# Pooling as fp32 products with averaging matrices, and rows of features turned on TensorE and fetched back from DRAM

## The chip, the cores and the metric

The kernel runs on one core of a Trainium2 chip. The metric is the device time in microseconds of one execution of the program; the time shown is the median of three runs. The profile is one further execution. TensorE appears as PE (matmuls) and PEld (weight loads), VectorE as DVE, ScalarE as ACT, GpSimd as POOL and SyncE as SP.

## The reference

Two small transformers follow one another on 256 tokens of 1024 features. The first has two layers (sparse attention, then differential attention) and a final norm, the second two layers: a pooling mixer, then block attention, each modulated by vectors that come from a conditioning vector `c` and the matrix `w_mod`. The change lies at the seam between them, in the pooling mixer and in what makes rows of modulation vectors:

```python
def modulate(h, shift, scale):
    return h * (1 + scale[:, None, :]) + shift[:, None, :]

def pool_mixer(h, w_pool, pool_scale):
    ...
    for g, w in enumerate(POOL_WINDOWS):          # 2, 4, 8, 16
        sl = slice(g * POOL_GROUP, (g + 1) * POOL_GROUP)
        cs_g = cs[:, :, sl]                       # running sums over tokens
        lo = jnp.maximum(t + 1 - w, 0)
        win_sum = cs_g[:, 1:] - jnp.take(cs_g, lo, axis=1)
        cnt = jnp.minimum(t + 1, w).astype(jnp.float32)[None, :, None]
        groups.append(win_sum / cnt - hf[:, :, sl])
    pooled = jnp.stack(groups, axis=2)
    y = jnp.einsum('bsgi,gio->bsgo', pooled, w_pool.astype(jnp.float32)).reshape(B, S, D)
    return (y * pool_scale.astype(jnp.float32)).astype(h.dtype)
```

Its input is the final norm of the first model, normed again and modulated; its output is multiplied by a gate and added to the stream `x`.

## The kernel before

Tokens lie in two tiles of 128 (`t`), features in 8 blocks of 128 (`b`). All weights come as one stream of 1 MB chunks through a ring of four buffers; SP issues the loads. ACT makes the upper half of each chunk (`whi`, `hi_upto`), DVE the remainder (`wlo`, `lo_upto`), and PE multiplies in three fp32r products (`three`, L1224). Nothing is scheduled by a planner: each engine's order is the order of its own program text, and semaphores join them.

The stages are: even mixer, MLP0, differential mixer, MLP1, pooling, MLP2, block-attention mixer, MLP3. Norms are numbered as events. Event 4 is the first model's final norm, event 5 the norm ahead of the pooling, event 6 the one ahead of MLP2, events 7 and 8 lie around the last mixer. In an event DVE adds the product to `x` (`residual`, L745, or L747 and L749 with a gate), ACT squares it (L446) and makes `std` (L451), DVE makes `rstd` (L756) and scales rows into `o_` (`scaled`, L762), PE transposes them (`norm`, L1307), ACT scales the features out of PSUM (`upper`, L463 or L465) and DVE splits them (`lower`, L775 and L776). `add_and_norm` (L778) does one tile and then the other.

The pooling stage: after events 4 and 5, PE transposes both tiles, ACT writes features into `qk` with gain and shift, and DVE adds shifted copies of them along the tokens (L1171, L1172), corrects the first tokens (L1175) and subtracts the token itself (L1176), group by group; ACT makes the upper part (L674), DVE the remainder (L1181, L1184), and PE multiplies by the pool's weights. Then follow two `wlo` splits, `mod_vectors(1)` (L820, L824), the residual of event 6 by halves, and its norm.

A vector over features lies as a column, [128, 8]. Where a row on all partitions is needed (the gates, and `cact`, by which DVE multiplies `w_mod` at L791 in MLP0 to MLP2), PE multiplies each broadcast column by the identity (`spread_col`, L1314), 8 fp32 products, and ACT copies two banks (`spread_copy`, L526). This stands in MLP0, MLP2 and MLP3, at the head of the last mixer, and for `gpool` in front of event 5's transposes. `w_mod` is loaded through POOL's queue (L411), one pair of buffers in turn.

## Time and profile before

| | |
|---|---|
| median of three runs | 1220.47 us (1219.09 to 1221.52) |
| profiled execution, its own time | 1216.48 us |
| its span, mean granted clock | 1214.6 us, 0.985 |
| PE busy | 1136.2 us, 94% |
| DVE busy | 812.5 us, 67% |
| ACT busy | 598.5 us, 49% |
| DMA | 248.57 MB, mean 205 GB/s |

The span is cut into 40 slices of 30.4 us. PE is at eight or nine tenths or more in nearly all; the lowest pair is slices 23 and 24 (5 and 6 tenths), where the granted clock is also lower (7 and 8 tenths): the pooling stage. "Clock" is the granted clock as a share of full speed: 1 is 2.4 GHz, 0.5 is 1.2 GHz. Matmul records overlap, so that their durations add up to more than the time they take; the distance between starts is what one costs.

### The profile page before, as it was taken

To read this page: it belongs to the slowest core of one execution; us is meant where nothing else is said; L and a number is where in the kernel's file an instruction comes from. 1 tells how busy PE (TensorE), PEld (TensorE's weight loads), DVE (VectorE), ACT (ScalarE), POOL (GpSimd) and SP (SyncE) were. 2 spreads that over 40 slices of the span, in tenths; PEclk is the share of its full clock that TensorE was granted. 3 is DMA by queue.
4 is the path that set the end of the run, shared out by engine and by line. 5 is a ranking of instruction groups with operands and counts; after the bars stand their busy time and mean duration, and the time that the engine had idled before them with its cause. 6 is when DMAs were issued, how large, how long until landed. Compare 5 with 4: busy or idle time off the path is not lost.

```text
span 1214.6 us, 17892 instructions
## 1 busy us (share of the span) xinstructions
PE 1136.2 (94%) x7264; PEld 986.2 (81%) x7264; DVE 812.5 (67%) x1342; ACT 598.5 (49%) x930; POOL 53.3 (4%) x103
## 2 busy tenths in 40 slices
PE   5898999999999999999999569999999998999997
...
DMA packets 36274, 248.57 MB, mean 205 GB/s; under 512 B 4560, under 2 KB 4704, under 8 KB 7520
## 3 DMA queue, kind: packets, MB, share of 16 engines
...
## 4 chain that ended last, share of the span: by engine, by line
PE 83%; DVE 10%; ACT 4%; issue 2%; DMA 1%; SPq 0%; DVEq 0%; ACTq 0%
PE bank L1229 71%; PE bank L1647 2%; PE bank L1411 2%; PE bank L1436 2%; DVE wlo L729 1%; PE bank L1474 1%; DVE x L749 1%; ACT vo L446 1%; DVE wlo L840 1%; DVE work L747 1%; PE bank L1307 1%; DVE ul L776 1%; PE bank L1630 1%; DMA raw<-in_stream 1%; PE bank L1711 1%
## 5 line engine op out<-in xcount | busy, mean ns | idle before, releaser
L729 DVE TENSOR_TENSOR wlo<-raw,whi 128x2048 fp32r<-128x2048 f32 (+2 forms) x143 | 324.5, 2274 | 108.2 <-ACT whi L436 108.1
L1229 PE MATMUL bank<-uh,whi 128*128 128x256 f32 x1272 | 367.4, 289 | 0.0
L1229 PE MATMUL bank<-ul,whi 128*128 128x256 f32 x1272 | 359.7, 283 | 0.0
L1229 PE MATMUL bank<-uh,wlo 128*128 128x256 f32 x1272 | 359.7, 283 | 0.0
L436 ACT ACTIVATE whi<-raw 128x2048 fp32r<-128x2048 f32 (+2 forms) x143 | 270.6, 1897 | 1.8 <-DMA raw<-in_stream 1.8
L1229 PEld LDWEIGHTS bank<-uh,whi 128*128 128x128 f32 x1272 | 243.5, 191 | 9.2 <-issue 6.7
L1229 PEld LDWEIGHTS bank<-ul,whi 128*128 128x128 f32 x1272 | 243.6, 192 | 4.0 <-issue 1.9
L1229 PEld LDWEIGHTS bank<-uh,wlo 128*128 128x128 f32 x1272 | 243.5, 191 | 0.0
L1229 PE MATMUL bank<-whi,hh 128*128 128x512 f32 x544 | 214.0, 393 | 0.0
L1229 PE MATMUL bank<-wlo,hh 128*128 128x512 f32 x544 | 212.4, 390 | 0.0
L1229 PE MATMUL bank<-whi,hl 128*128 128x512 f32 x544 | 211.8, 389 | 0.0
L494 ACT ACTIVATE hh<-work 128x512 fp32r<-128x512 f32 x56 | 35.4, 632 | 173.2 <-PE bank L1229 173.2
L1229 PEld LDWEIGHTS bank<-whi,hl 128*128 128x128 f32 x544 | 102.1, 188 | 21.8
L1229 PEld LDWEIGHTS bank<-whi,hh 128*128 128x128 f32 x544 | 102.4, 188 | 20.9 <-issue 1.6
L490 ACT ACTIVATE work<-bank 128x512 f32<-128x512 f32 x56 | 33.5, 598 | 174.1 <-PE bank L1229 174.1
L1229 PEld LDWEIGHTS bank<-wlo,hh 128*128 128x128 f32 x544 | 102.4, 188 | 18.8 <-issue 0.2
L791 DVE CUSTOM_DVE_ANT_0 qk<-qk,cb 128x1024 f32<-128x1024 f32 x96 | 113.1, 1221 | 0.0
L1229 PE MATMUL bank<-whi,uh 128*128 128x256 f32 (+2 forms) x256 | 88.4, 345 | 19.6 <-DVE ul L776 10.1
L805 DVE TENSOR_TENSOR work<-work 128x512 f32<-128x512 f32 x56 | 38.7, 691 | 74.5 <-ACT work L490 74.5
L1229 PE MATMUL bank<-wlo,uh 128*128 128x256 f32 (+2 forms) x256 | 85.1, 332 | 0.0
L1229 PE MATMUL bank<-whi,ul 128*128 128x256 f32 (+2 forms) x256 | 85.0, 332 | 0.0
L840 DVE TENSOR_TENSOR wlo<-raw,whi 128x1024 fp32r<-128x1024 f32 x56 | 67.4, 1219 | 8.5 <-ACT whi L617 8.4
(205 smaller groups left out, 1118.2 us busy)
## 6 DMA issues: line engine op xcount, KB each, us to landing
...
bias_rows<-gb POOLq DMA_DIRECT2D x16, 192.0 KB, 9.1
...
x<-in_x SPq DMA_DIRECT2D x2, 512.0 KB, 4.7
vo<-in_fin_g POOLq DMA_DIRECT2D x2, 512.0 KB, 6.7
out_y<-vo SPq DMA_DIRECT2D x2, 512.0 KB, 2.6
```

The costliest lines, as they stand in the source:

```text
L436: nc.scalar.activation(whi[:, c % RING, 0:w], raw[:, n % RING, 0:w], ACT.Copy).then_inc(hi_ready, 1)
L446: nc.scalar.activation(o_[:, t, 512 * h:512 * h + 512], x[:, t, 512 * h:512 * h + 512], ACT.Square, accum_out=ss[:, 2 * t + h:2 * t + h + ...
L490: nc.scalar.activation(work[:, s % 2, :], bank[s % 2][:, :], ACT.Relu).then_inc(relu_done, 1)
L494: nc.scalar.activation(hh[:, s % 2, :], work[:, s % 2, :], ACT.Square).then_inc(hh_done, 1)
L729: nc.vector.tensor_tensor(wlo[:, c % RING, 0:w], raw[:, raw_index(c) % RING, 0:w], whi[:, c % RING, 0:w].bitcast(fp32), ALU.subtract).then ...
L791: ins = nc.vector.tensor_tensor_reduce(out=stage[j][:, r, :], in0=stage[j][:, r, :], in1=cb[:, :], scale=1.0, scalar=0.0, op0=ALU.mult, op ...
L805: nc.vector.tensor_tensor(work[:, 2 + s % 2, :], work[:, s % 2, :], work[:, s % 2, :], ALU.mult)\
L840: ins = nc.vector.tensor_tensor(wlo[:, m % RING, c], raw[:, raw_index(m) % RING, c], whi[:, m % RING, c].bitcast(fp32), ALU.subtract)
L1229: ins = mm(out, st, mv, start=start and i == 0, stop=stop and i == 2, skip_group_check=True)
L1411: ins = mm(bank[3 + c][:, c0:c1], qk[rows_, qb, 128 * t:128 * t + 128], qk[rows_, kb, 0:c1 - c0], start=True, stop=True)
L1436: ins = nc.tensor.transpose(bank[5][:, 128 * k:128 * k + 128], P[:, (2 * p + c) % 4, 128 * k:128 * k + 128], ident)
L1647: ins = mm(bank[acc_of(1)[2 * t + h]][:, :], oT[c][:, k, 128 * t:128 * t + 128], w[:, k, 512 * h:512 * h + 512], start=c == 0 and k == 0, ...
```

## The change

**Pooling.** The averaging over the window, less the token itself, becomes a matrix over tokens. For each of the four groups it is made on the host (`pool_windows`, 128x1152 in all), with the part that carries the last tokens of tile 0 into the first 16 of tile 1. PE multiplies the normalised rows of a tile by it as plain fp32, 8 products of 128 columns a tile and 8 of 16 columns from tile 0 into tile 1, which turns rows into features at the same time. The gain is put on by DVE as it writes the rows (`pool_input`); the shift only matters where a row of the matrix does not sum to nought, the first tokens, and comes as 8 products of one row by 16 columns. The transposes of event 5, the 16 ACT copies into `qk` and DVE's chain of adds go. ACT and DVE take halves of each tile out of PSUM (`pooled_upper`, `pooled_lower`). Tile 0 is done ahead of tile 1, also in the product with the pool's weights and in event 6, which is now `add_and_norm(6, gateb)`. `mod_vectors(1)` moves ahead of event 4; one of the two `wlo` splits stays ahead of event 6, the other moves behind it.

**Rows.** A column is turned by one PE transpose into 8 rows of 128 (three columns in MLP1: `gpool`, the pooling's gain and shift), copied by ACT into `rowb`, written to DRAM and fetched on all partitions by POOL's queue. `cact` is turned in the even mixer, and `gpool` in MLP1.

```diff
-            def spread_col(col, b0):
-
-                for b in range(KB):
-                    ins = mm(bank[b0 + b // 4][:, 128 * (b % 4):128 * (b % 4) + 128],
-                             col[:, b:b + 1].to_broadcast([128, 128]), ident, start=True, stop=True)
-                ins.then_inc(spread, 1)
+            def turn_columns(*cols):
+
+                for n, col in enumerate(cols):
+                    ins = nc.tensor.transpose(bank[6][0:8, 128 * n:128 * n + 128], col, ident)
+                ins.then_inc(row_ps, 1)
...
-            def spread_copy(k, dst, b0):
-                act.wait_ge(spread, k + 1)
-                for j in range(2):
-                    nc.scalar.activation(dst[:, 512 * j:512 * j + 512], bank[b0 + j][:, :], ACT.Copy).then_inc(spread_out, 1)
+            def turned_columns(k, n=1):
+                act.wait_ge(row_ps, k + 1)
+                if k:
+                    act.wait_ge(row_out[k - 1], 16)
+                nc.scalar.activation(rowb[:, 0:n, :], bank[6][0:8, 0:128 * n].rearrange("p (n f) -> p n f", n=n), ACT.Copy)\
+                    .then_inc(row_sb, 1)
...
+            def rows_to(k, n=1):
+
+                pool.wait_ge(row_sb, k + 1)
+                pool.dma_start(rdram[k, 0:n, :].rearrange("n (b p) -> b n p", p=128), rowb[:, 0:n, :]).then_inc(row_out[k], 16)
+
+            def row_from(k, dst, n=0):
+
+                pool.wait_ge(row_out[k], 16)
+                pool.dma_start(dst, rdram[k, n, :].partition_broadcast(128)).then_inc(row_in[k], 16)
...
+                    pool.dma_start(win[:, 0:W_END], a["windows"]).then_inc(in_win, 16)
...
+                    if m == 1 and i == 2:
+                        rows_to(1, 3)
+                    elif m == 1 and i == 4:
+                        row_from(1, gateb)
+                        row_from(1, gain_row, 1)
+                        pool.dma_start(shift_row, rdram[1, 2:3, :]).then_inc(row_in[1], 16)
+                    elif m == 2 and i == 2:
+                        rows_to(2)
+                    elif m == 2 and i == 4:
+
+                        pool.wait_ge(x_ready, x_no(6, 1, 1))
+                        row_from(2, gateb)
...
-            for t in range(NT):
-                deviation(4, (t,))
-                deviation(5, (t,))
-            spread_copy(1, gateb, 2)
-            act.wait_ge(mod_ready, 1)
-            for t in range(NT):
-                upper(5, t, gain[:, 0, :], mod[:, 0:8], qk[:, 0:8, :])
-            hi_upto(POOL + 3)
-            for g in range(4):
-                act.wait_ge(p_sum, g + 1)
-                nc.scalar.activation(uh[:, 2 * g:2 * g + 2, :], u[:, 2 * g:2 * g + 2, :], ACT.Copy).then_inc(p_hi, 1)
-            deviation(6, halves=(0,))
-            deviation(6, halves=(1,))
+            def pooled_upper(t):
+
+                for h in range(2):
+                    act.wait_ge(p_sum, 2 * t + h + 1)
+                    nc.scalar.activation(uh[:, 4 * h:4 * h + 4, 128 * t:128 * t + 128],
+                                         bank[2 * t + h][:, :].rearrange("p (b n) -> p b n", b=4), ACT.Copy).then_inc(p_hi, 1)
+
+            deviation(4, (0,))
+            deviation(5, (0,))
+            deviation(4, (1,))
+            pooled_upper(0)
+            deviation(5, (1,))
+            pooled_upper(1)
+            hi_upto(POOL + 2)
             act.wait_ge(mod_ready, 2)
             for t in range(NT):
+                deviation(6, (t,))
                 upper(6, t, gain[:, 1, :], mod[:, 24:32])
+            hi_upto(POOL + 3)
             mlp(2)
             for t in range(NT):
...
+            mod_vectors(1)
+            dve.wait_ge(row_in[1], 48)
+
+            def pool_input(t):
+
+                inverse(5, t)
+                for q in range(4):
+                    c = slice(256 * q, 256 * q + 256)
+                    nc.vector.scalar_tensor_tensor(out=o_[:, t, c], in0=x[:, t, c], scalar=rstd[:, t:t + 1], in1=gain_row[:, c],
+                                                   op0=ALU.mult, op1=ALU.mult).then_inc(xs_ready, 1)
+
+            def pooled_lower(t):
+                for h in range(2):
+                    dve.wait_ge(p_hi, 2 * t + h + 1)
+                    us_ = slice(4 * h, 4 * h + 4), slice(128 * t, 128 * t + 128)
+                    nc.vector.tensor_tensor(ul[:, us_[0], us_[1]], bank[2 * t + h][:, :].rearrange("p (b n) -> p b n", b=4),
+                                            uh[:, us_[0], us_[1]].bitcast(fp32), ALU.subtract).then_inc(p_h, 1)
+
             for t in range(NT):
                 residual(4, (t,))
                 inverse(4, t)
                 gained(4, t, x, x_ready)
-                scaled(5, t)
-
-            hb, sa = qk[:, 0:8, :], qk[:, 8:16, :]
-            sbb = P[:, :, :].rearrange("p a n -> p (a n)").rearrange("p (b n) -> p b n", n=T)
-            dve.wait_ge(un_ready, un_no(6, 0))
-            for g, w in enumerate((1, 2, 4, 8)):
-                n = 8 - 2 * g
-                src = (hb, sa[:, 2:8, :], sbb[:, 2:6, :], sa[:, 6:8, :])[g]
-                dst = (sa, sbb, sa[:, 4:8, :], sbb[:, 4:6, :])[g]
-                nc.vector.tensor_copy(dst[:, 0:n, 0:w], src[:, 0:n, 0:w])
-                link(nc.vector.tensor_tensor(dst[:, 0:n, w:T], src[:, 0:n, w:T], src[:, 0:n, 0:T - w], ALU.add))
-
-                cor = con[:, C_CORR + 32 * g:C_CORR + 32 * g + 32].rearrange("p (b n) -> p b n", b=2)
-                link(nc.vector.tensor_tensor(dst[:, 0:2, 0:16], dst[:, 0:2, 0:16], cor, ALU.mult))
-                nc.vector.scalar_tensor_tensor(out=u[:, 2 * g:2 * g + 2, :], in0=dst[:, 0:2, :],
-                                               scalar=1.0 / (2 << g), in1=hb[:, 2 * g:2 * g + 2, :],
-                                               op0=ALU.mult, op1=ALU.subtract).then_inc(p_sum, 1)
-                if g:
-                    dve.wait_ge(p_hi, g)
-                    nc.vector.tensor_tensor(ul[:, 2 * g - 2:2 * g, :], u[:, 2 * g - 2:2 * g, :],
-                                            uh[:, 2 * g - 2:2 * g, :].bitcast(fp32), ALU.subtract).then_inc(p_h, 1)
-            dve.wait_ge(p_hi, 4)
-            nc.vector.tensor_tensor(ul[:, 6:8, :], u[:, 6:8, :], uh[:, 6:8, :].bitcast(fp32), ALU.subtract).then_inc(p_h, 1)
-            lo_upto(POOL + 3)
-            mod_vectors(1)
-            dve.wait_ge(spread_out, 4)
-            residual(6, halves=(0,), gate=gateb)
-            residual(6, halves=(1,), gate=gateb)
-            for t in range(NT):
-                scaled(6, t)
-            for t in range(NT):
-                lower(6, t)
+                if t:
+                    pooled_lower(0)
+                pool_input(t)
+            pooled_lower(1)
+            lo_upto(POOL + 2)
+            add_and_norm(6, gateb)
...
-                if l == 0:
-                    pe.wait_ge(col_ready, 2)
-                    spread_col(cact, 6)
+                if l == 1:
+                    pe.wait_ge(mod_ready, 1)
+                    turn_columns(gpool[:, :], gain[:, 0, :], mod[:, 0:8])
                 elif l == 2:
                     pe.wait_ge(mod_ready, 2)
-                    spread_col(mod[:, 40:48], 6)
+                    turn_columns(mod[:, 40:48])
                 elif l == 3:
                     pe.wait_ge(mod_ready, 3)
-                    spread_col(mod[:, 88:96], 6)
+                    turn_columns(mod[:, 88:96])
...
-                if l != 1:
-                    pe.wait_ge(spread_out, (2, 0, 6, 10)[l])
+                if l:
+                    pe.wait_ge(row_sb, (0, 2, 3, 5)[l])
...
-            pe.wait_ge(mod_ready, 1)
-            spread_col(gpool, 2)
-            pe.wait_ge(spread_out, 4)
-            for t in range(NT):
-                norm(5, t)
-
+
+            pe.wait_ge(in_win, 16)
+            pe.wait_ge(row_in[1], 48)
+
+            for b in range(KB):
+                c = W_SUM + WIDEST * (b // 2)
+                mm(bank[b // 4][:, 128 * (b % 4):128 * (b % 4) + WIDEST], shift_row[0:1, 128 * b:128 * b + 128],
+                   win[0:1, c:c + WIDEST], start=b % 4 == 0, stop=False, skip_group_check=True)
+
+            def pooled(t, c0, n, to=None):
+
+                to = t if to is None else to
+                for b in range(KB):
+                    if b % 2 == 0:
+                        pe.wait_ge(xs_ready, 4 * (dg_no(5, t) - 1) + b // 2 + 1)
+                    c = W_GROUP * (b // 2) + c0
+                    ins = mm(bank[2 * to + b // 4][:, 128 * (b % 4):128 * (b % 4) + n], o_[:, t, 128 * b:128 * b + 128],
+                             win[:, c:c + n], start=to > t and b % 4 == 0, stop=True, skip_group_check=True)
+                    if b % 4 == 3 and to == t:
+                        ins.then_inc(p_sum, 1)
+
+            pooled(0, 0, 128)
+            pooled(0, W_NEXT, WIDEST, 1)
             pe.wait_ge(lo_ready, POOL + 1)
             wp = [w[:, POOL % RING, :].rearrange("p (g k n) -> p g k n", g=4, k=2) for w in (whi, wlo)]
-            for g in range(4):
-                pe.wait_ge(p_h, g + 1)
-                for t in range(NT):
-                    ts = slice(128 * t, 128 * t + 128)
+            for t in range(NT):
+                ts = slice(128 * t, 128 * t + 128)
+                if t:
+                    pooled(1, W_SECOND, 128)
+                for g in range(4):
+                    pe.wait_ge(p_h, 2 * t + g // 2 + 1)
                     for k in range(2):
                         ins = three(bank[4 + 2 * t + g // 2][:, 256 * (g % 2):256 * (g % 2) + 256], False,
                                     wp[0][:, g, k, :], wp[1][:, g, k, :], uh[:, 2 * g + k, ts], ul[:, 2 * g + k, ts],
                                     g % 2 == 0 and k == 0, g % 2 == 1 and k == 1)
-                    if g == 1 or (g == 3 and t == 0):
+                    if g % 2 and (t, g) != (1, 3):
                         ins.then_inc(acc_ready, 1)
             ins.then_inc(used, 1)
...
+def pool_windows():
+    win = np.zeros((128, W_END), np.float32)
+    s, t = np.arange(T)[:, None], np.arange(T)[None, :]
+    for g in range(4):
+        w = 2 << g
+        weight = np.where((t >= s) & (t - s < w), np.float32(1) / np.minimum(t + 1, w).astype(np.float32), np.float32(0))
+        weight = weight - np.eye(T, dtype=np.float32)
+        c = W_GROUP * g
+        win[:, c:c + 128] = weight[:128, :128]
+        win[:, c + W_NEXT:c + W_SECOND] = weight[:128, 128:128 + WIDEST]
+        win[:, c + W_SECOND:c + W_GROUP] = weight[128:, 128:]
+
+        win[0, W_SUM + WIDEST * g:W_SUM + WIDEST * g + WIDEST] = weight.astype(np.float64).sum(0)[:WIDEST]
+    return win```

The order of the instructions, at three places. First DVE around the end of event 5, before: the rows `vo` of tile 1, then the adds along the tokens (`qk` and `P` are scratch for features).

```order
L753 TENSOR_SCALAR bias<-ss 128x1
L756 RECIPROCAL rstd<-std 128x1
L762 TENSOR_SCALAR vo<-x,rstd 128x256 x4
L1171 COPY qk<-qk 128x8
L1172 TENSOR_TENSOR qk<-qk 128x8x255
L1175 TENSOR_TENSOR qk<-qk,con 128x2x16
L1176 SCALAR_TENSOR_TENSOR u<-qk 128x512
L1171 COPY P<-qk 128x6x2
L1172 TENSOR_TENSOR P<-qk 128x6x254
L1175 TENSOR_TENSOR P<-P,con 128x2x16
L1176 SCALAR_TENSOR_TENSOR u<-P,qk 128x512
L1181 TENSOR_TENSOR ul<-u,uh 128x512
```

And DVE now, from tile 1's residual of event 4 to the first gate product of event 6 (`work<-bank,vo`):

```order
L797 TENSOR_TENSOR x<-bank,x 128x512 x2
L805 TENSOR_SCALAR bias<-ss 128x1
L808 RECIPROCAL rstd<-std 128x1
L819 SCALAR_TENSOR_TENSOR x<-x,rstd,vo 128x512 x2
L1225 TENSOR_TENSOR ul<-bank,uh 128x4x128 x2
L805 TENSOR_SCALAR bias<-ss 128x1
L808 RECIPROCAL rstd<-std 128x1
L1218 SCALAR_TENSOR_TENSOR vo<-x,rstd,u 128x256 x4
L1225 TENSOR_TENSOR ul<-bank,uh 128x4x128 x2
L781 TENSOR_TENSOR wlo<-raw,whi 128x2048
L799 TENSOR_TENSOR work<-bank,vo 128x512
L801 TENSOR_TENSOR x<-work,x 128x512
```

The remainder of tile 0 stands between tile 1's two norms, and one `wlo` stands ahead of the gate product. Second, PE at the end of MLP1, before (`con` holds the identity):

```order
L1229 MATMUL bank<-wlo,hh 128x512
L1229 MATMUL bank<-whi,hl 128x512
L1314 MATMUL bank<-con,gpool 128x128 x8
L1307 MATMUL bank<-con,vo 128x128 x16
L1229 MATMUL bank<-whi,uh 128x256
```

And now (`P` holds the window matrices, `u` the row of shifts, `vo` the rows of a tile):

```order
L1273 MATMUL bank<-wlo,hh 128x512
L1273 MATMUL bank<-whi,hl 128x512
L1788 MATMUL bank<-P,u 128x16 x8
L1798 MATMUL bank<-P,vo 128x128 x8
L1798 MATMUL bank<-P,vo 128x16 x8
L1273 MATMUL bank<-whi,uh 128x256
```

The spread and the 16 transposes are replaced by three sets of eight; a fourth set, tile 1's, stands behind tile 0's 24 products with the pool's weights. Third, POOL's queue from the even mixer's end to MLP2, before:

```order
L411 DMA qk<-in_w_mod 128x2048 x16
L400 DMA bias_rows<-gb 128x1x384 x16
L406 DMA vo<-in_fin_g 128x1024
L411 DMA qk<-in_w_mod 128x2048 x32
L418 DMA u<-bias_rows 128x256 x16
```

And now, for MLP1's part:

```order
L433 DMA vo<-in_fin_g 128x1024
L434 DMA P<-in_windows 128x1152
L451 DMA qk<-in_w_mod 128x2048 x2
L395 DMA feature_rows<-rowb 8x3x128
L451 DMA qk<-in_w_mod 128x2048 x2
L400 DMA vo<-feature_rows 128x1024
L400 DMA u<-feature_rows 128x1024
L442 DMA u<-feature_rows 1x16x64
L451 DMA qk<-in_w_mod 128x2048 x14
```

The write of the rows stands behind the first pair of `w_mod` loads, the three fetches behind the second.

## Rows read from the trace of the kernel before

**Rows 1.** The page's chain that ended last: shares of the span by engine

```profile
PE 83%; DVE 10%; ACT 4%; issue 2%; DMA 1%; SPq 0%; DVEq 0%; ACTq 0%
```

**Rows 2.** Waits of PE over the span: us in total, times, longest

```profile
PE bank L1307 <- DVE vo L762: 27.8, 11, 8.8
```

**Rows 3.** Timeline of PE, pooling stage: start, us, engine, line, op, tiles, count, [idle before]

```profile
671.27 1.95 PE L1314 MATMUL bank<-con,gpool 128*128 128x128 f32 x16
677.96 4.49 PE L1307 MATMUL bank<-con,vo 128*128 128x128 f32 x16 [4.74 <-ACT vo L526]
691.21 0.55 PE L1229 MATMUL bank<-whi,uh 128*128 128x256 f32 x1 [8.77 <-DVE ul L1181]
...
708.00 1.97 PE L1307 MATMUL bank<-con,vo 128*128 128x128 f32 x8 [8.79 <-DVE vo L762]
```

**Rows 4.** Windows there: us, busy us of each engine, then clock, DMA share, GB/s

```profile
671.30:678.00 6.70, 1.96 (x18) 1.77 (x16) 4.70 (x15) 4.28 (x12) 0.00 (x0) 0.92 0.00 1
678.00:682.50 4.50, 4.33 (x16) 2.68 (x16) 0.30 (x2) 3.76 (x11) 0.00 (x0) 0.50 0.00 0
```

**Rows 5.** Timeline of DVE, pooling stage

```profile
665.27 1.45 DVE L745 TENSOR_TENSOR x<-bank,x 128x512 f32<-128x512 f32 x2
...
668.04 1.41 DVE L767 SCALAR_TENSOR_TENSOR x<-x,rstd,vo 128x512 f32<-128x512 f32 x2
...
670.77 1.14 DVE L762 TENSOR_SCALAR vo<-x,rstd 128x256 f32<-128x256 f32 x4
...
696.74 4.49 DVE L729 TENSOR_TENSOR wlo<-raw,whi 128x2048 fp32r<-128x2048 f32 x2
701.14 0.18 DVE L820 TENSOR_TENSOR mod<-modr,con 128x32 f32<-128x32 f32 x1
```

**Rows 6.** Timeline of ACT, pooling stage

```profile
667.51 0.30 ACT L451 ACTIVATE std<-ss,bias 128x1 f32<-128x1 f32 x1
...
684.24 3.80 ACT L436 ACTIVATE whi<-raw 128x2048 fp32r<-128x2048 f32 x2
```

**Rows 7.** The chain in order of time, head of MLP2, last mixer: start, us, what

```profile
722.47 1.78 PE bank L1314 x16
724.25 5.75 PE bank L1229 x48
...
912.86 2.05 PE bank L1314 x16
```

**Rows 8.** Timeline of PE in the even mixer: eight fp32 products of 30 columns

```profile
102.71 1.97 PE L1583 MATMUL bank<-kcm,qk 128*128 128x30 f32 x16
```

**Rows 9.** Timelines of ACT and DVE, MLP2: copies out of PSUM

```profile
730.48 1.09 ACT L484 ACTIVATE hh<-bank 128x512 fp32r<-128x512 f32 x2 [0.25 <-PE bank L1345]
...
731.11 1.29 DVE L798 TENSOR_TENSOR hl<-bank,hh 128x512 fp32r<-128x512 f32 x2 [1.61 <-ACT hh L484]
```

**Rows 10.** Timelines of DVE, ACT, PE and the chain, event 8 ahead of MLP3

```profile
1012.60 0.69 DVE L747 TENSOR_TENSOR work<-bank,cb 128x512 f32<-128x512 f32 x1 [0.85 <-PE bank L1229]
...
1022.43 0.68 DVE L747 TENSOR_TENSOR work<-bank,cb 128x512 f32<-128x512 f32 x1
...
1016.12 1.28 ACT L451 ACT_TABLE_LOAD   x1
...
1020.56 0.36 PE L1229 MATMUL bank<-whi,uh 128*128 128x256 f32 x1 [0.98 <-DVE ul L776]
...
1028.12 5.74 PE bank L1229 x48
```

**Rows 11.** The page's DMA issues: tiles, queue, op, count, KB each, us to landing

```profile
bias_rows<-gb POOLq DMA_DIRECT2D x16, 192.0 KB, 9.1
...
vo<-in_fin_g POOLq DMA_DIRECT2D x2, 512.0 KB, 6.7
```

**Rows 12.** Timelines of POOL and DVE, MLP1: first loads of w_mod and their use

```profile
486.17 1.06 POOL L411 DMA_DIRECT2D qk<-in_w_mod  x2
...
515.00 1.22 DVE L791 CUSTOM_DVE_ANT_0 qk<-qk,cb 128x1024 f32<-128x1024 f32 x1
```

63 lines of the change are left out of this document (41 added, 22 removed).

## The prediction

> **What bounds the kernel now.** I read the views from the whole to the place. The chain of waits gives TensorE 83% of the span and VectorE 10% [rows 1]: what shortens TensorE's own stream, or a stretch in which it stands still, shortens the kernel. The list of TensorE's waits names the largest: 27.8 us in 11 times before transposes L1307, for the normalised rows that DVE writes at L762 [rows 2]. TensorE's timeline shows that the longest stand around the pooling: after `spread_col(gpool)` at 671.27 it stands 4.74 us, after the 16 transposes of event 5 it stands 8.77 us until 691.21, and before the transposes of event 6 (708.00) another 8.79 us [rows 3]. The windows show it as clock too: 0.92 from 671.3 to 678, 0.50 in the next 4.5 us [rows 4]; with levels of 1 and 0.5, 0.92 means a fall near 676.9, some 4 us after the last spread. So the stage from 671.3 to the product at 724.25 [rows 7], 53 us, is one of hand-offs, not of TensorE work.
>
> **The pooling stage, worked out on the old time axis.** DVE's split of the pool's weights ends near 665.3. It then makes `mod_vectors(1)`, which is moved here: it starts at 701.14 before, 0.18 us and two smaller products, 0.46 with their starts [rows 5]. The first residual starts at 665.73 instead of 665.27, but its second half had to wait for TensorE until 666.03 anyway, so 0.3 us is lost. Gained rows start 0.3 later than 668.04 [rows 5], event 5's `rstd` is there at 671.05. The four 128x256 writes L762 took 1.14 us; now they are scalar_tensor_tensor with the gain row. For their price the nearest row is L767, 1.41 us for as many elements in two instructions; 1.14 is the lower end and 1.9 (two more starts and a slower form) an upper end; I take 1.5. Tile 0 is ready at 672.55.
>
> TensorE meanwhile makes 8 fp32 products of one row by 16 columns, from 671.27. An fp32 product shows as two records; eight with 30 columns (L1583) are 16 records in 1.97 us, the last of them 0.27 long, so starts 0.113 apart [rows 8], and eight with 128 columns are 1.78 us in the chain [rows 7]: the width hardly counts, so each new set of eight costs 1.8 us. Bounds are 0.9 and 3.6 us (half, as if the weight load went for nothing, and double, at the lower clock). The sets: 673.05; the product of tile 0 until 674.85; the 16-column set into tile 1 until 676.6. ACT's second half of a norm takes 1.08 us from DVE's last write to `std` (666.73 to 667.81, [rows 6] has its last row), so `std` of tile 1's event 4 comes at 674.95; DVE starts the gained rows at 675.15 and ends at 676.4. ACT copies the pooled tile 0 out of PSUM in two halves, priced by `hh<-bank`, 1.09 us for two [rows 9]: 676.05. DVE's remainders are priced by `hl<-bank`, 1.29 for two [rows 9]: first half 677.05, second 677.65. TensorE makes 24 fp32r products of tile 0, starts 0.12 apart: 680.0. DVE makes tile 1's input from 678.3 to 679.85; TensorE's product of tile 1 ends at 681.8, ACT's copy at 682.45, DVE's remainder at 683.15, the last 24 products at 685.2.
>
> Now a wait appears that the order shows: DVE has one `wlo` (POOL+2) ahead of the residual, and ACT issues its `whi` only behind the pooled copies. By 3.80 for two [rows 6] it ends at 684.3; by 4.49 for two [rows 5] `wlo` ends at 686.6. That is what is late next, and the residual of event 6 starts at 686.65. From here event 8 is the model, as it has the same `add_and_norm` with a gate ahead of an MLP: first L747 at 1012.60, first product 1020.56, 7.96 us, of which 1.28 is a table load that doesn't fall in here [rows 10]. So the first product of MLP2 comes at 693.3. Second tile: in event 8 its L747 starts 9.83 us after the first's, 8.53 without the table load, and the products behind its transposes count from 1028.12, 5.69 later [rows 10]: 700.9. TensorE stands for some 3 us ahead of these transposes, as it did in event 8; before it didn't, since both tiles' residuals were already made. 48 products at 5.75 us [rows 7]: 706.6. One transpose of a 128x8 column, 0.11 to 0.2 us, takes the place of the 1.78 us spread. The product that started at 724.25 [rows 7] starts at 706.8. **Stage: -17.4 us.** The first third of MLP2's tile 0 at the lower clock is in both kernels and hides behind DVE in the new one.
>
> **The other spreads.** The same 1.78 us in the chain stands ahead of MLP0's and MLP3's last opening products (three such pieces in all, one shown), and 2.05 us in the last mixer [rows 7], where TensorE had waited for DVE's gain. Behind each, TensorE runs without a gap for many us, so they are worth their length: MLP0 -1.78 (its transpose moves into the even mixer, +0.15), mixer -1.85, MLP3 -1.65. MLP1 had no spread in it and gets three transposes, +0.33. ACT's two copies of 1.1 us become one small copy of about 0.3; in MLP1 it is one more, hidden, since DVE and TensorE don't wait for it before `down(0)`. **Together -4.8 us.**
>
> **What I cost at nothing.** Fetching a row back is a broadcast of 512 KB; `in_fin_g` has that shape and landed in 6.7 us [rows 11]. All five are asked for tens of us before their reader. On POOL's queue each `rows_to` stands in front of loads of `w_mod` that must wait for DVE's `st_done` anyway, and the fetches stand behind the pair before. The window matrices (576 KB) delay the first `w_mod` pair of MLP1 by 1 to 2 us; it is asked for at 486.17 and DVE takes it at 515.00 [rows 12]. If that cover were gone, MLP1 would lose up to 2 us. The wait for `gb` and `cact` ahead of the first transpose is for small work at the start of DVE's order, ahead of its first rotation of features.
>
> **Sum.** -17.4 - 4.8 = -22.2 us against the profiled execution: 1216.48 becomes 1194.3. That execution lies 4.0 us below the median of the runs, 1220.47; the same loss from the median gives **1198.3 us**.
>
> **Rivals.**
> (a) The clock falls within the stage. Before, TensorE was 4.33 us busy of 4.50 by the records from 678 with sparse transposes, and its clock stayed at 0.50 [rows 4]; the new stream has gaps of about 0.6 us and sets with 16 columns. For it to stay at 1 speaks that L1583's row, products as thin as these, ran at the short pitch of 0.113 [rows 8]. Falling from the first product on, the sets and the 24s double: outer and first product end at 678.4, the 16 columns at 682, tile 0's 24 at 687, tile 1's product at 690.7 instead of 681.8. Everything behind moves by 8.8 us: -13.4 in all, 1207. Falling from 677 on: about 5 us, 1203.
> The Trainium skill, "TensorE: Matmul & The Clock Gate", section "A second HAM failure mode: psum-queue depth-cycling", says that a TensorE that idles briefly and often between groups of matmuls swings between its two clock levels. By that rule this stage would be the place for it and the time rival (a)'s, 1203 to 1207; by the row of L1583 it is the forecast's. I give the rule 12 in 100.
> (b) The spreads outside the stage are worth nothing, because DVE or a transfer is next in line at the head of the MLPs. Then 5.3 us of the gain is missing: 1203.6. Against it: ACT copies the spread too, so ACT and DVE also move up.
> (c) Slower. The fetched rows behave like `bias_rows<-gb`, 192 KB in 9.1 us [rows 11], not like `in_fin_g`. At that rate 512 KB needs 24.3 us. In MLP1 two come behind one another, 48.6 us, on POOL's queue ahead of the next `w_mod`; DVE waits for that load with the splits of the stream queued behind it, and TensorE waits for the splits. One more stands in MLP2's loads. Uncovered that is 73 us: 1271; it decides against the change once more than 22 us of it are left uncovered. For it: the queue is in order. Against it: the slow transfer has DRAM as its target and one partition as its source, the fetches neither.
> (d) The change doesn't do what it says, the pooling chain being only traded for waits on `whi` and PSUM copies: the hi-lo hand-off of each tile would have to cost 17 us more than its rows. 1 in 100, within 0.2% of before.
>
> **How the numbers follow.** Forecast 74 in 100 (1198.3, by itself 1194.5 to 1201.5, from the bounds 1.14 to 1.9, twice, the sets at half price, hand-offs of some tenths each), (a) 12, (b) 10, (c) 3, (d) 1. Faster: 96 less a little for causes not seen, 95; slower 3; same 2. About 0.2% (2.4 us) is what a measurement of this kernel can tell from no change. The range reaches over (b) and the milder (a), 1194 to 1205.5.
>
> **What would show it.** Right: in the new profile TensorE's stand of 8.8 us before the pooling's products is gone; the clock is 1 from the end of MLP1 until the last pooling product; DVE's first gate product of event 6 starts 21 us or so behind the first residual of event 4, with `whi` as what ended the idle time before its `wlo`; the first product of MLP2 comes 22 us behind the end of MLP1, where before even the transposes ahead of it started 37 us behind (708.00, [rows 3]); 3 us of idle before event 6's second transposes. Wrong: a clock of 0.5 within the stage (a), TensorE idle at the head of an MLP that had none (b), DVE waiting for a transfer at the `w_mod` products of MLP1 (c).

## The result, and the profile of the changed kernel

The changed kernel takes **1199.32 us** (median; 1199.16 to 1201.50), the kernel before 1220.05 in the same comparison (1219.09 to 1221.52): a ratio of 0.9835, 95% interval 0.9818 to 0.9851, or 20.7 us less. The forecast was 1198.3 us, 22.2 less. The profiled execution took 1199.16 us, its span 1197.4.

The page's chain by engine hardly moved against [rows 1], and TensorE's waits for the normalised rows fell by 2.9 us only (its name L1351 was L1307, [rows 2]):

```profile
PE 84%; DVE 9%; ACT 4%; issue 2%; DMA 1%; SPq 0%; DVEq 0%; ACTq 0%
```
```profile
PE bank L1351 <- DVE vo L814: 24.9, 12, 6.9
```

The place tells more than the totals. This is the chain of the changed kernel in order of time (start, us, what), from the first residual of event 4 to the product behind MLP2's single transpose, with the short pieces left out:

```profile
666.69 0.61 DVE x L797
...
671.96 1.67 DVE vo L1218 x4
...
677.57 0.61 DVE ul L1225
...
678.32 3.10 PE bank L1273 x24
681.42 1.80 PE bank L1798 x16
...
683.74 1.91 ACT whi L481
...
685.68 2.29 DVE wlo L781
687.97 0.61 DVE work L799
...
701.14 1.92 PE bank L1351 x8
703.06 6.50 PE bank L1273 x48
709.56 0.11 PE bank L1358
709.67 5.75 PE bank L1273 x48
```

Up to 677.57 it is VectorE and ScalarE: the pooling products of tile 0 don't appear, since they run beside tile 1's residual. At 683.74 `whi`, at 685.68 `wlo` stand in the chain, as the "late next" of the prediction, then event 6's residual. TensorE's timeline and its windows there (columns as in [rows 3, 4]; the windows are of TensorE alone):

```profile
672.32 1.95 PE L1788 MATMUL bank<-P,u 1*128 1x16 f32 x16
674.20 3.74 PE L1798 MATMUL bank<-P,vo 128*128 128x128 f32 x32
678.32 0.36 PE L1273 MATMUL bank<-whi,uh 128*128 128x256 f32 x1 [0.37 <-DVE ul L1225]
...
683.73 0.39 PE L1273 MATMUL bank<-whi,uh 128*128 128x256 f32 x1 [0.52 <-DVE ul L1225]
...
692.35 1.97 PE L1351 MATMUL bank<-con,vo 128*128 128x128 f32 x8 [5.49 <-DVE vo L814]
694.81 0.55 PE L1273 MATMUL bank<-whi,uh 128*128 128x256 f32 x1 [0.49 <-DVE ul L828]
...
701.14 1.92 PE L1351 MATMUL bank<-con,vo 128*128 128x128 f32 x8 [1.90 <-DVE vo L814]
```
```profile
672.30:681.00 8.70, 8.33 (x71) 1.00 0.00 0
681.00:687.00 6.00, 5.34 (x44) 1.00 0.01 3
687.00:692.40 5.40, 0.06 (x1) 0.87 0.76 272
692.40:697.90 5.50, 5.00 (x23) 0.51 0.72 305
700.00:704.50 4.50, 3.36 (x16) 0.64 0.00 0
```

Against [rows 3] the stands of 4.74 and 8.77 us are gone, with 0.37 and 0.52 us left ahead of the two sets of 24 products; one of 5.49 stands where 8.79 was, and 1.90 us are new before the second transposes. MLP1 ends where the first set of this stage begins (672.32 here). Granted clock: 1 through all pooling products, 0.51 and 0.64 in event 6, which is the lower of two levels for most of it.

To compare executions without what happens elsewhere I use one length throughout: **from MLP1's turning of its squares to MLP2's** (transposes L1388, in the kernel before L1345, first start to first start). Its value is 224.5 us before (505.32 to 729.84) and 209.0 in the changed kernel (506.27 to 715.26): 15.5 us less.

### The profile page after: what moved, and what is told of

Same layout as the page of the kernel before. It is cut to its first block, busy times and chain, and to the rows that moved or that the text cites. A ratio compares the mean times of both kernels' runs of the same rounds, so it can differ in the third digit from the quotient of the medians.

```text
span 1197.4 us, 17819 instructions
## 1 busy us (share of the span) xinstructions
PE 1137.2 (95%) x7239; PEld 988.0 (83%) x7239; DVE 804.0 (67%) x1326; ACT 588.5 (49%) x909; POOL 60.3 (5%) x116
## 4 chain that ended last, share of the span: by engine, by line
PE 84%; DVE 9%; ACT 4%; issue 2%; DMA 1%; SPq 0%; DVEq 0%; ACTq 0%
PE bank L1273 73%; PE bank L1690 2%; PE bank L1454 2%; PE bank L1479 2%; PE bank L1517 1%; PE bank L1351 1%; DVE x L801 1%; DVE ul L828 1%; ACT vo L491 1%; DVE wlo L892 1%; PE bank L1673 1%; DVE work L799 1%; PE bank L1758 1%; DMA raw<-in_stream 1%; DVE wlo L781 1%
## 5 line engine op out<-in xcount | busy, mean ns | idle before, releaser
L781 DVE TENSOR_TENSOR wlo<-raw,whi 128x2048 fp32r<-128x2048 f32 (+2 forms) x143 | 324.5, 2273 | 99.1 <-ACT whi L481 99.1
L1273 PE MATMUL bank<-uh,whi 128*128 128x256 f32 x1272 | 368.7, 290 | 0.0
L1273 PE MATMUL bank<-ul,whi 128*128 128x256 f32 x1272 | 360.8, 284 | 0.0
L1273 PE MATMUL bank<-uh,wlo 128*128 128x256 f32 x1272 | 360.7, 284 | 0.0
L481 ACT ACTIVATE whi<-raw 128x2048 fp32r<-128x2048 f32 (+2 forms) x143 | 270.4, 1894 | 0.9 <-DMA raw<-in_stream 0.9
L1273 PEld LDWEIGHTS bank<-uh,whi 128*128 128x128 f32 x1272 | 244.7, 192 | 9.4 <-issue 6.7
L1273 PEld LDWEIGHTS bank<-ul,whi 128*128 128x128 f32 x1272 | 244.7, 192 | 4.1 <-issue 1.9
L1273 PEld LDWEIGHTS bank<-uh,wlo 128*128 128x128 f32 x1272 | 244.6, 192 | 0.0
L1273 PE MATMUL bank<-whi,hh 128*128 128x512 f32 x544 | 214.0, 393 | 0.0
L1273 PE MATMUL bank<-wlo,hh 128*128 128x512 f32 x544 | 212.4, 390 | 0.0
L1273 PE MATMUL bank<-whi,hl 128*128 128x512 f32 x544 | 211.8, 389 | 0.0
L1273 PEld LDWEIGHTS bank<-whi,hl 128*128 128x128 f32 x544 | 102.1, 188 | 22.0
L1273 PEld LDWEIGHTS bank<-whi,hh 128*128 128x128 f32 x544 | 102.4, 188 | 20.8 <-issue 1.6
L1273 PEld LDWEIGHTS bank<-wlo,hh 128*128 128x128 f32 x544 | 102.4, 188 | 18.9 <-issue 0.2
L843 DVE CUSTOM_DVE_ANT_0 qk<-qk,cb 128x1024 f32<-128x1024 f32 x96 | 113.1, 1218 | 2.1 <-DMA qk<-in_w_mod 2.1
L1273 PE MATMUL bank<-whi,uh 128*128 128x256 f32 (+2 forms) x256 | 89.7, 350 | 10.0 <-DVE ul L828 8.9
L1273 PE MATMUL bank<-wlo,uh 128*128 128x256 f32 (+2 forms) x256 | 86.0, 336 | 0.0
L1273 PE MATMUL bank<-whi,ul 128*128 128x256 f32 (+2 forms) x256 | 86.0, 336 | 0.0
L892 DVE TENSOR_TENSOR wlo<-raw,whi 128x1024 fp32r<-128x1024 f32 x56 | 67.4, 1218 | 6.9 <-ACT whi L666 6.8
## 6 DMA issues: line engine op xcount, KB each, us to landing
bias_rows<-gb POOLq DMA_DIRECT2D x16, 192.0 KB, 9.4
vo<-feature_rows POOLq DMA_DIRECT2D x3, 512.0 KB, 8.6
x<-in_x SPq DMA_DIRECT2D x2, 512.0 KB, 5.0
cb<-feature_rows POOLq DMA_DIRECT2D x2, 512.0 KB, 4.9
```

Source lines behind the costliest of these rows:

```text
L481: nc.scalar.activation(whi[:, c % RING, 0:w], raw[:, n % RING, 0:w], ACT.Copy).then_inc(hi_ready, 1)
L781: nc.vector.tensor_tensor(wlo[:, c % RING, 0:w], raw[:, raw_index(c) % RING, 0:w], whi[:, c % RING, 0:w].bitcast(fp32), ALU.subtract).then ...
L843: ins = nc.vector.tensor_tensor_reduce(out=stage[j][:, r, :], in0=stage[j][:, r, :], in1=cb[:, :], scale=1.0, scalar=0.0, op0=ALU.mult, op ...
L892: ins = nc.vector.tensor_tensor(wlo[:, m % RING, c], raw[:, raw_index(m) % RING, c], whi[:, m % RING, c].bitcast(fp32), ALU.subtract)
L1273: ins = mm(out, st, mv, start=start and i == 0, stop=stop and i == 2, skip_group_check=True)
```

## The experiments

All twelve are timed beside the kernel before on the same chip. The traces are read from one execution of each.

**The same two kernels again.**

> The kernel before, unchanged, for a second profile of it. Theory: its profiled execution of 1216.48 us was a few us under its other runs (1219.1 to 1221.5) because the granted clock in the even mixer happened to stay up; I expect the median at 1220 us, ratio 1.000, and in the new profile a granted clock that differs in a few windows of the even mixer or of the pooling stage and accounts for the difference of the two spans. Rival: 1216.5 is what it takes when profiled, and the second profile gives the same 1214.6 us span.

> The changed kernel, unchanged, for a second profile of it. Expected median 1199.3 us, ratio 0.983 (-20.7 us). Theory on the 1.9 us that my forecast of the pooling stage missed: they are event 6's transposes and first MLP2 products at the lower level of the clock; if the second profile shows the clock at 1 there, the stage (from MLP1's last product to MLP2's turning of its squares) is 1.9 us shorter, if it shows 0.5 again the same 43.0 us. Theory on the even mixer: the fall of the clock at 36.7 to 40 us (2.4 us later at the end) is not the change's and can be absent from this profile.

Before: 1219.64 us median over 12 runs (1217.33 to 1222.43), ratio 1.0001 [0.9989, 1.0013], span 1215.5. Changed: 1197.59 (1196.23 to 1200.19), ratio 0.9821 [0.9801, 0.9842]. The runs of one kernel follow the mean granted clock of each roughly: in the kernel before 1222.43, 1219.76 and 1221.21 us come with 0.979 (but 1219.51 with 0.977), 1217.33 and 1217.5 with 0.983, and the execution of 1216.48 that the prediction was worked on had 0.985. So that one was no other kernel, only one with fewer falls of the clock. In this second profile of before the fall near 130 us is missing, and others stand near 414 and 1028. Both profiled executions of before are among its fastest.

The second profile of the changed kernel shows what the prediction had as rival (a). TensorE's timeline and windows in the pooling stage:

```profile
671.36 1.95 PE L1788 MATMUL bank<-P,u 1*128 1x16 f32 x16
673.24 6.09 PE L1798 MATMUL bank<-P,vo 128*128 128x128 f32 x32
...
684.43 1.99 PE L1798 MATMUL bank<-P,vo 128*128 128x128 f32 x16
686.94 0.38 PE L1273 MATMUL bank<-whi,uh 128*128 128x256 f32 x1 [0.52 <-DVE ul L1225]
...
695.57 1.97 PE L1351 MATMUL bank<-con,vo 128*128 128x128 f32 x8 [5.50 <-DVE vo L814]
```
```profile
671.30:675.00 3.70, 3.70 (x29) 0.90 0.00 0
675.00:683.00 8.00, 8.00 (x40) 0.50 0.00 0
```

The 32 records of L1798 take 6.09 us instead of 3.74, tile 0's 24 products come at half pace, and the length is 211.7 us instead of 209.0. The clock fell here under a TensorE that the records show busy without a gap. Event 6's second transposes were at full clock this time (1.23 us instead of 1.92), and the chain shows what that is worth: from their start to the 48 products' end it takes 6.98 us instead of 8.42.

```profile
704.36 1.23 PE bank L1351 x8
705.59 5.75 PE bank L1273 x48
```

I expected that the fall of the clock in the even mixer, 2.4 us later in the first profile, was not the change's and could be absent. It was not absent. These are the windows of TensorE from 35 to 43 us in `before_again`, `after_again` and `pool_only` (below), whose even mixer stands as before:

```profile
35.00:43.00 8.00, 7.11 (x53) 1.00 0.87 294
```
```profile
35.00:43.00 8.00, 6.58 (x42) 0.79 0.76 257
```
```profile
35.00:43.00 8.00, 6.51 (x40) 0.79 0.82 255
```

Both profiles of before have 1.00 there, and all twelve profiles of kernels with any part of the change have 0.57 or 0.79. From the second transposes at the head of the even mixer (18.03 us in the changed kernel) to the next ones that read `con` and `vo` (121.63) it takes 99.40 us in both profiles of before and 101.0 to 103.6 in the other twelve. TensorE stands for 2.92 us ahead of this place in before and changed kernel alike. Whether the change brings this fall, or the two profiled executions of before were without it by chance, is not shown.

**The two halves of the change apart.** `rows_only` is the kernel before with four of its spreads turned into rows; `pool_only` is the changed kernel with those four put back:

```
 (rows_only, from before; the same for MLP0, the last mixer and MLP3)
-                    spread_col(mod[:, 40:48], 6)
+                    turn_columns(mod[:, 40:48])
 (pool_only, from the changed kernel: the reverse)
```

> The kernel before with four of its five spreads (MLP0, MLP2, second mixer, MLP3) replaced by a transposed row sent through memory; the pooling stage stays as before, with its own spread. Theory (each spread stands on PE's path): MLP0 -1.8, MLP2 -1.8, mixer -1.0 to -1.85, MLP3 -1.7, +0.15 for the even mixer's transpose: -6.1 to -7.0 us, so 1213 to 1214 us. Rival (the spreads lie in slack): within 1 us of 1220.

> The changed kernel with the four other spreads put back (MLP0, MLP2, second mixer, MLP3), the pooling stage as changed. Theory: what is left of the 20.7 us after 6.1 to 7.0 us for the rows: -13.7 to -14.6 us against the kernel before, so 1205.4 to 1206.4 us; the two parts add up. Rival (spreads worth nothing): -20 us, 1200 us. A third possibility is that a longer PE row of work in event 6 keeps the clock up there; then this one loses less, -16 us.

Rows alone: 1214.24 us, ratio 0.9953 [0.9936, 0.9970], -5.6, half a microsecond short of what was expected. Pooling alone: 1205.83, ratio 0.9883 [0.9864, 0.9901], -14.0, as expected. Together -19.6, the whole -20.7 and -22.2: they add up within what the intervals allow, and rival (b) falls. By place, in the traces: the length of above goes from 224.5 to 222.7 for the rows alone (MLP2's spread, -1.8) and to 210.7 for the pooling alone; MLP3's head (second transposes of event 8 to MLP3's turning) from 14.35 to 12.67 in the changed kernel, and where the clock fell in it from 15.84 (`before_again`) to 14.15 (`rows_only`), so -1.7 either way; the last mixer (second transposes of event 7 to those of event 8) from 124.1 to 123.1.

That last one is 1.0 where 1.85 was forecast. In `after_again` it is 122.3, so 1.8. The difference of 0.75 us comes with a granted clock of 0.6 in the first 4 us behind event 7's second transposes, which `rows_only` and the first profile of the changed kernel have and `after_again` hasn't.

**The tile order of event 6, undone.**

```
-            add_and_norm(6, gateb)
+            residual(6, gate=gateb)
+            for t in range(NT):
+                scaled(6, t)
+            for t in range(NT):
+                lower(6, t)
```
(and on ScalarE both deviations ahead of both upper parts)

> The changed kernel with event 6's steps of VectorE and ScalarE put back into the order of before: residual of both token tiles, then both scaled, then both lowered, instead of one tile after the other. Theory (the tile order is part of the gain: tile 0's first products run while tile 1 is being normalised): in the changed kernel tile 0's transposes start 4.5 us after the first gated residual, here the second residual (2.7 us) stands ahead of them; MLP2's first product comes 2.7 us later and PE is then not held for tile 1; from the last pooling product to MLP2's turning of its squares 1 us more to 1 us less than in the changed kernel, time 1198 to 1200.5 us. Rival (tile order is where much of the gain lies): 3 us slower than the changed kernel, 1202 us.

1202.55 us (1198.06 to 1203.27), ratio 0.9841 [0.9821, 0.9861]; the length is 209.3. In its profile the clock fell to 0.66 from 675 to 680 us, which put the last 24 pooling products 1.1 us later (12.5 us behind MLP1's end instead of 11.4); from them to MLP2's turning it takes 30.7 us instead of 31.5. The median is the number of the rival, but its step, 3 us more behind the pooling products, is not there; other falls of the clock are, near 133 and 416 us and two behind 1007. Turning tile by tile in event 6 brings nothing: what tile 0 gains, tile 1 pays behind it. The gain of the stage lies in the pooling itself.

**The split that was late next.**

```
             pooled_upper(0)
             deviation(5, (1,))
-            pooled_upper(1)
             hi_upto(POOL + 2)
+            pooled_upper(1)
...
-            pooled_lower(1)
             lo_upto(POOL + 2)
+            pooled_lower(1)
```

> The changed kernel with one weight piece (number POOL+2) split ahead of tile 1's upper and lower parts, on ScalarE in its idle 3.1 us after its last square and on VectorE in its idle 1.9 us, instead of after them. Theory (the split, 2.3 us of VectorE plus 1.1 us of wait for ScalarE, is what is late next between the last pooling product and event 6): the first gated residual starts about 0.3 us after the last pooling product's end is seen by VectorE instead of 0.9 us behind it; the last pooling products come 0.4 us later because VectorE's lower part waits for the split; -0.3 to -1 us against the changed kernel. Rival (VectorE was free for 2.3 + 1.1 us that all lay on the path): -3 us, 1195.5 us.

1197.87 us, ratio 0.9819 [0.9799, 0.9840]; length 205.4, **3.6 us less** than the changed kernel's. The rival was right, and my expectation had a fault: the first gated residual is of tile 0 and needs nothing of tile 1's products, so it does not wait for their end (it starts at 684.79, while they run until 687.2). The median shows 1.5 us of it, or nothing against `after_again`; its profile gives 1.5 us back in MLP3's head (14.1 us instead of 12.67, clock 0.62 behind event 8's second transposes).

**The two tiles woven.** On top of the split:

```
-            add_and_norm(6, gateb)
+            residual(6, (0,), gate=gateb)
+            residual(6, (1,), (0,), gate=gateb)
+            scaled(6, 0)
+            residual(6, (1,), (1,), gate=gateb)
+            lower(6, 0)
+            scaled(6, 1)
+            lower(6, 1)
```
(and on ScalarE the square of tile 1's first half ahead of tile 0's upper part)

> The changed kernel with the split of the piece before as early, and event 6's two token tiles woven on VectorE: residual(0), first half of residual(1), scaled(0), second half of residual(1), lower(0), scaled(1), lower(1); on ScalarE the square of tile 1's first half comes before tile 0's upper part. Theory (event 6 is bounded by VectorE's chain of two tiles with its waits for ScalarE, 1.05 us for a deviation and 0.8 us for an upper part in each tile, and PE only follows): tile 0's residual starts 3 us earlier, in the wait for tile 1's pooling products, tile 1's chain no longer stands behind tile 0's lower part; MLP2's 48 products for tile 1 start 4 to 5 us earlier: 1194 to 1195.5 us. Rival (PE's own work and the clock bound it): within 1 us of the changed kernel.

**1191.57 us** (1189.25 to 1193.01), ratio 0.9762 [0.9744, 0.9779], length 204.0: the best of all, 28.9 us under the kernel before and below the interval of the changed kernel. Expected were 1194 to 1195.5: the length has 5.0 us of the gain over the changed kernel, and the medians 6.0 to 7.8. Its timeline of TensorE:

```profile
687.53 1.23 PE L1359 MATMUL bank<-con,vo 128*128 128x128 f32 x8 [2.49 <-DVE vo L816]
690.39 0.55 PE L1281 MATMUL bank<-whi,uh 128*128 128x256 f32 x1 [1.64 <-DVE ul L830]
690.75 0.42 PE L1281 MATMUL bank<-wlo,uh 128*128 128x256 f32 x1
690.96 0.41 PE L1281 MATMUL bank<-whi,ul 128*128 128x256 f32 x1
...
695.65 1.09 PE L1359 MATMUL bank<-con,vo 128*128 128x128 f32 x8
```

Ahead of the second transposes TensorE no longer waits for VectorE. The 24 products of tile 0 now end only at 695.65, 0.213 us apart, at the lower level of the clock; VectorE had the second tile's rows ready at 693.3.

**TensorE kept at work.** Products of the identity by itself, written to a bank that nobody reads:

```
             ins.then_inc(used, 1)
+            for n in range(40):
+                mm(bank[2][:, 0:128], ident, ident, start=True, stop=True)
             norm(6, 0)
...
                 first(0, 0)
+                for n in range(12 if l == 2 else 0):
+                    mm(bank[2][:, 128:256], ident, ident, start=True, stop=True)
                 norm(e, 1)
```

> The changed kernel with products that nobody reads (128x128 fp32 identity by identity, one every 0.11 to 0.12 us at full clock) in PE's idle time of event 6: 40 after the last pooling product (of 5.5 us idle), 12 between tile 0's first products and tile 1's transposes (of 1.9 us idle). They take PE's time where it waits for VectorE anyhow. Theory (1.9 us of the stage are the clock's fall in that idle time): granted clock 1 from the last pooling product to MLP2's turning of its squares, transposes 1.23 us for eight instead of 1.97, the 24 and 48 products 0.12 us apart throughout, and 1.5 to 2 us less: 1197.3 us against 1199.3, in the profile 41.0 to 41.5 us from MLP1's last product to MLP2's turning against 42.9. Rival (a fall for another reason, or products that come too late and hold the transposes up): no gain, or up to 1 us slower.

1199.68 us, ratio 0.9832 [0.9817, 0.9847]. The clock stayed at 1.00 in every window of the stage, but each product took twice as long as I had counted:

```profile
686.53 9.10 PE L1823 MATMUL bank<-con 128*128 128x128 f32 x80
695.46 1.04 PE L1351 MATMUL bank<-con,vo 128*128 128x128 f32 x8
```

80 records for 40 products: the transposes waited for them until 695.46. From there to MLP2's turning it took 21.2 us instead of 22.9, so the clock's share is 1.7 us, and the delay ate it. Hence the next, with 20 and 7:

> The changed kernel with unread products again, but 20 and 7 of them: the run before showed each 128x128 fp32 product recorded twice, 0.2275 us together, so 40 of them took 9.1 us in a gap of 5.5 and held the transposes up; 20 take 4.55 us and 7 take 1.6. Theory (the clock's fall in PE's idle time of event 6 is the 1.9 us missed): no hold, the granted clock stays 1 from the last pooling product on, and from tile 1's last 24 pooling products to MLP2's turning of its squares it takes 29.7 us instead of 31.5 (in the run with 40 products it took 21.2 us from tile 0's transposes instead of 22.9); time 1196.5 to 1198 us. Rival: the clock is not what it hangs on, 31.5 us again.

1196.80 us (1196.44 to 1201.10), ratio 0.9824 [0.9807, 0.9841]; length 207.3, **1.7 us less** than the changed kernel's, and 29.85 us from the last pooling products to MLP2's turning, for which 29.7 were expected, against 31.53:

```profile
686.82 4.63 PE L1823 MATMUL bank<-con 128*128 128x128 f32 x40
692.48 1.22 PE L1351 MATMUL bank<-con,vo 128*128 128x128 f32 x8 [1.03 <-DVE vo L814]
694.70 0.55 PE L1273 MATMUL bank<-whi,uh 128*128 128x256 f32 x1 [1.00 <-DVE ul L828]
...
699.11 1.73 PE L1413 MATMUL bank<-con 128*128 128x128 f32 x14
701.02 1.23 PE L1351 MATMUL bank<-con,vo 128*128 128x128 f32 x8 [0.19 <-DVE vo L814]
```
```profile
694.60:698.20 3.60, 3.50 (x17) 0.53 0.60 250
```

The term missed in the forecast is this one. The clock did not stay at 1 as expected: it fell from 694.6 on, behind two stands of 1.0 us, but only over tile 0's first products, whose length VectorE hides, and it was back for the second transposes. And the same in the woven kernel, 9 products before and 5 behind tile 0's transposes:

> The woven kernel (1191.6 us) with 9 unread products (2.05 us at full clock) in PE's idle 2.5 us ahead of tile 0's transposes and 5 (1.14 us) in its idle 1.6 us behind them. In the woven kernel the 24 first products of MLP2 are 0.213 us apart (granted clock 0.5 from 690 to 695 us) and end at 695.65, where tile 1's transposes could have started at 693.3. Theory: clock 1 there, 24 products in 2.9 us, tile 1's transposes 2.3 us earlier, 1189.3 us, the best version of this study. Rival: the products push the transposes back by what they overrun, within 0.5 us of the woven kernel.

1194.11 us (1191.86 to 1195.00), ratio 0.9795 [0.9782, 0.9808], where 1189.3 was expected: **slower** than woven, whose interval lies just below. Yet its profile shows the forecast step to the tenth: tile 1's transposes at 693.72, length 201.8, 2.2 us less than woven's. The rest of that execution gave it back, 0.8 us between the second transposes of event 7 and those of event 8, 1.5 in MLP3's head; and it was the fastest of its five runs, at a mean clock of 0.993, the others at 0.989 or 0.990 where woven's had 0.992 or 0.993. Holding the clock up in one place did not hold it up in the whole. What links the places was not found.

**Each row fetched three times**, every fetch behind the arrival of the one before:

```
                 pool.wait_ge(row_out[k], 16)
-                pool.dma_start(dst, rdram[k, n, :].partition_broadcast(128)).then_inc(row_in[k], 16)
+                for j in range(3):
+                    if n or j:
+                        pool.wait_ge(row_in[k], 48 * n + 16 * j)
+                    pool.dma_start(dst, rdram[k, n, :].partition_broadcast(128)).then_inc(row_in[k], 16)
```

> The changed kernel with each spreading fetch of a row (1x1024 in memory to 128x1024) done three times, one behind the other's arrival, on the same queue, so that each row arrives some 17 to 20 us later (8.6 us from issue to landing each in the changed kernel's trace) and GpSimd's later issues come later too. Theory (the rows are well covered): MLP0's, MLP2's, mixer's and MLP3's rows have over 20 us in hand; GpSimd's fetches of the modulation weights in MLP1 and MLP2 are held up by 35 and 18 us, which VectorE may feel in its own slack; within 2 us of 1199.3. Rival (the fetch lies near the path): the wait for the row or for the weights reaches PE, 5 to 20 us slower.

1210.89 us (1209.37 to 1213.65), ratio 0.9934 [0.9920, 0.9948]: 11.6 us slower than the changed kernel's 1199.32. The rival held. GpSimd's, VectorE's and TensorE's timelines in MLP1:

```profile
521.10 0.53 POOL L403 DMA_DIRECT2D vo<-feature_rows  x1
530.10 0.53 POOL L403 DMA_DIRECT2D vo<-feature_rows  x1 [8.47 <-DMA vo<-feature_rows]
...
550.68 1.07 POOL L454 DMA_DIRECT2D qk<-in_w_mod  x2
```
```profile
557.05 1.23 DVE L846 CUSTOM_DVE_ANT_0 qk<-qk,cb 128x1024 f32<-128x1024 f32 x1 [20.00 <-DMA qk<-in_w_mod]
...
559.95 2.28 DVE L784 TENSOR_TENSOR wlo<-raw,whi 128x2048 fp32r<-128x2048 f32 x1
```
```profile
562.29 0.80 PE L1276 MATMUL bank<-whi,hh 128*128 128x512 f32 x1 [7.57 <-DVE wlo L784]
```

The rows themselves have time; the loads of `w_mod` queued behind them have not. The next pair is issued at 550.68, VectorE waits 20.00 us for it with the splits of the stream behind it, and TensorE 7.57 for the split. Of the 11.6 us, 9.5 are in MLP1, from its turning to its end. In the changed kernel the same wait of VectorE is 2.1 us in all, 1.3 of them in MLP0 and 0.8 in MLP1, and none in the trace of before; MLP1 takes the same from its turning to its end, 166.0 us in both:

```profile
L843 DVE CUSTOM_DVE_ANT_0 qk<-qk,cb 128x1024 f32<-128x1024 f32 x96 | 113.1, 1218 | 2.1 <-DMA qk<-in_w_mod 2.1
```

**Without the shift's products.** This kernel leaves the shift of the pooling's norm out of the output:

```
-            for b in range(KB):
-                c = W_SUM + WIDEST * (b // 2)
-                mm(bank[b // 4][:, ...], shift_row[0:1, ...], win[0:1, c:c + WIDEST], ...)
```

> The changed kernel without the eight products of one row each that add the shift's share to the first 16 tokens (the shift of the pooling norm is left out of the output). Naive reading of my own sum: the set took 1.8 to 1.9 us of PE's time at the head of the stage, so -1.8 us. Theory from the trace of the changed kernel: VectorE sets the pace there (its scaling of tile 0, both residuals and tile 0's lower part follow each other without a wait for PE), so the 24 first pooling products still wait for VectorE's lower part and nothing is gained: 0 to -0.3 us, 1199 us; the stage from MLP1's last product stays at 43 us.

1199.92 us, ratio 0.9844 [0.9829, 0.9859]; length 210.2. Nothing is gained. The gap moves to behind the product of tile 0:

```profile
670.42 3.72 PE L1793 MATMUL bank<-P,vo 128*128 128x128 f32 x32 [0.20 <-DVE vo L1218]
676.14 0.55 PE L1273 MATMUL bank<-whi,uh 128*128 128x256 f32 x1 [2.01 <-DVE ul L1225]
```

With 2.01 us of idle time ahead of them the 24 products start at the lower clock (0.53 from 675 to 680), and the length is 1.2 us *more* than with the eight.

## Why the prediction was right, and where it was off

- **TensorE's stands in the stage are the reserve.** Right: -15.5 us of the 17.2 between the first two profiles lie between the two turnings (-12.8 between the second two, with rival (a)'s fall in it), and `pool_only` is 14.0 us faster by itself.
- **The steps up to event 6.** The changed trace starts this stage 1.05 us later than the axis of the prediction. With that taken off, forecast and measured are: tile 0's first of 24 products 677.1 and 677.27, tile 1's product ended 681.8 and 682.2, `wlo` ended 686.6 and 686.9, with the first gate product right behind it in both. The four scaled writes took 1.67 us, not 1.5. The wait on `whi` and `wlo` was there as named, and `split_early` shows it worth 3.6 us. Two slips of the sum are small: the gained rows, priced at 1.41 us, are given 1.25, and 9.83 less 1.28 is 8.55, not 8.53.
- **What the sets of eight are worth.** The price was right, 1.88 us of start to start for the outer products (forecast 1.8). "Each new set of eight costs 1.8 us" was not: in the sum itself tile 0's product ends 0.1 us ahead of ScalarE's `std`, beside the path, and `no_shift` shows the set of the shifts free. Only tile 1's set stands in the chain.
- **The term that was too small: event 6 by the model of event 8.** Forecast from the first gate product to the 48 products' end 19.95 us (686.65 to 706.6), measured 21.59 (687.97 to 709.56 in the chain). Event 8's clock was at 1 ahead of these products, and event 6 comes behind a stand of 5.5 us. Both its transposes (1.97 and 1.92 us for eight instead of 1.23) and the products behind each ran at the lower level, the 48 in 6.50 us instead of 5.75. I had written that the first third of tile 0 at the lower clock "hides behind DVE". Nearly: from the gate product to the second transposes it takes 13.17 us, about 0.2 more than in event 8 before, its table load taken off. The second stand, 1.90 us, had its own fall, which I had not costed, and it has 1.4 of the 1.6 us: 8.42 us from the second transposes to the 48 products' end, 6.98 in `after_again`, where the clock was up. `short_busy`, with the clock up at both transposes, gives 1.7 us back.
- **The signs.** DVE's first gate product starts 21.3 us behind the first residual of event 4 (forecast 21 or so), `whi` ended the idle time before its `wlo` (1.11 us), and MLP2's first product comes 22.5 us behind the end of MLP1 (forecast 22). Ahead of event 6's second transposes are 1.90 us of idle time and not 3: the 24 products ahead of them ran at half pace.
- **The other spreads, -4.8.** Right in kind: MLP0 -1.8, MLP3 -1.7, MLP1 +0.3 as forecast; the mixer -1.0 or -1.8, as the clock goes behind event 7.
- **Rival (a)** had 12 in 100 and was seen in the second profile of the changed kernel: 15.6 us from the first outer product to the last 24 pooling products instead of 11.4, a price of 4.2 us where 5 to 8.8 were forecast, since the clock came back some 10 us later; 2.7 of it are left in the length. A rival with a chance belongs to single executions here, not to the kernel. Of the ten profiles in which TensorE has this stream, three show such a fall (`after_again`, `both_tiles`, `rows_thrice`); in the first two the records show TensorE busy from MLP1's end up to it, so the short stands of the stage (0.37 and 0.52 us) had not come yet. The Trainium skill's rule on a TensorE that idles briefly and often ("TensorE: Matmul & The Clock Gate", section "A second HAM failure mode: psum-queue depth-cycling") is therefore not what those two show. Nearer is what the Trainium skill says in the same page, section "What's actually happening", of a kernel's start: one and the same kernel has a different number of slow matmuls from run to run. Here it is so in the middle of a kernel. What brings the clock down under a busy TensorE stays open; no run tells whether the sets of 16 columns or one row have a part in it.
- **Rival (c)** had its mechanism, the queue behind the fetches, and a price far too high. The 512 KB fetches land in 4.0 to 10.5 us by the changed kernel's trace, near `in_fin_g` [rows 11] and far from 24, and all is covered. The queue behind them is what would break first, as `rows_thrice` shows.
- **The sum against the median, and luck.** Against the profiled execution the sum said -22.2, and between the two profiled executions it is -17.2. By place, forecast and measured: even mixer +0.15 and +2.4, MLP0 -1.8 and -1.8, MLP1 +0.3 and +0.3, the stage -17.4 and -15.5, the last mixer -1.85 and -1.0, MLP3 -1.65 and -1.7. So the sum missed 5 us of this pair: 2.2 in the even mixer, where no fall of the clock was costed, 1.9 in the stage, 0.85 in the mixer. That the median came within 1.0 us of the forecast, and -20.7 near -22.2, is in part luck: the other executions of the kernel before lose more than the profiled one did, and no trace shows where. Taking the loss off the median was the better choice of the two.
